# Wide units of a two-block transformer kernel: the 512-column matmuls with the high weights first, then the 256-column matmuls with the low weights

## The chip, the cores and the metric

The kernel runs on one core of a Trainium2 chip, as one launch. The metric is the device time of that launch in microseconds (us), read as the median of several runs. The kernel before took 1072.92 us (median of 3 runs, 1071.69 to 1077.14).

## What is computed

Two blocks follow each other on a sequence of 256 tokens of width 1024, all in float32. The first has a convolution and neighbourhood attention side by side, an output projection and a gated feed-forward part. The second has two layers, each with attention over selected keys, a short convolution, gates, a mixing projection and a squared-ReLU feed-forward part. The parts that matter here are the feed-forward ones:

```python
def first_block(...):
    ...
    x = x + mix @ w_out[l]
    h = rms_norm(x, norm2_g[l])
    x = x + (jax.nn.silu(h @ w_gate[l]) * (h @ w_up[l])) @ w_down[l]   # 1024 -> 2816 -> 1024
    return x

def second_block(...):
    for l in range(DEPTH_2):                                          # 2 layers
        ...
        x = x + merged @ w_mix_out[l]
        u = rmsnorm(x, norm_mlp[l])
        x = x + jnp.square(jax.nn.relu(u @ w_mlp_up[l])) @ w_mlp_down[l]   # 1024 -> 4096 -> 1024
    return rmsnorm(x, norm_final)
```

## The kernel before

**Units.** All weights pass through the core once, in units of 1 MB: 128 partitions by 2048 floats. SyncE's queue loads a unit into one of 6 buffers `raw`. ScalarE (ACT in the profile) rounds it to `whi` (L982, in the tensor engine's float32 format), and VectorE (DVE) subtracts that from the raw weights and writes the rest to `wlo` (L1289). Both have 3 buffers. A weight is then whi + wlo, and an activation is treated in the same way: `uhl` holds, for each of 8 feature chunks f, 256 columns of high parts (tokens, `uhi`) and behind them 256 columns of low parts (`ulo`). A product is the sum of three: high times high, high times low and low times high.

**Semaphores.** `w_hi` counts the units that ScalarE has split, `w_lo` those that VectorE has. `used` counts the units that the tensor engine (PE) has finished; ScalarE waits for it before it overwrites a buffer, three units later. A load waits for `w_lo` of the unit six before. `u_lo` counts the low parts of activation chunks.

**Kinds of units.** Most units are multiplied by three matmuls a step (`mm3`, L513 to L515). Where a unit has 256 output columns ("col" units) each matmul has 256 columns; in the output projections and in the second half of the feed-forward parts ("rows" units, `acc` banks) each has 512 columns, 24 matmuls a unit. A third kind, the **wide unit**, is used for gate and up projections: L541 multiplies `whi` by all 512 columns of `uhl` at once, which gives high times high in the left half of a bank and high times low in its right half, and L542 multiplies `wlo` by the 256 high columns into the left half. One unit is 2 output chunks c by 8 features f, so 16 pairs of such matmuls, in the order c, f, L541, L542. ScalarE then copies the right half out and VectorE adds the left one.

There are 54 wide units, 864 pairs. In the first block units `A_FF` and `A_FF + 1` are gate and up of the first 256 hidden features; then `ff_block` runs ten times (gate, up, and a rows unit `down`), and a last rows unit follows. In each of the two layers `L_MLP` is the first wide unit, and `block` runs 15 times (a wide unit `up` and a rows unit `down`).

**Where a feed-forward part starts.** The first wide unit of each (`wide_features_after`) is multiplied while the normed activations are still being made: the tensor engine transposes a quarter of x (`turn_quarter`, L609), ScalarE scales and rounds it (L999), and VectorE makes its low part (L1314), 4 chunks a quarter. The last quarter is transposed after the first four features of chunk c = 0, and features 4 to 7 wait for `u_lo`. The next work of ScalarE is the split of the next unit or two, then the sums of squares (L1011). In the first block, the second wide unit has in its middle, between c = 0 and c = 1, the four matmuls of `spread_rn` (L636). They wait for `diag_ok` of VectorE, which stands behind ScalarE's square root, and behind VectorE's splits of two units.

Every engine takes its work in the written order. The waits of a wide unit in the kernel before are at its callers, ahead of all its matmuls:

```python
                pe.wait_ge(w_lo, gate.upto())
                pe.wait_ge(ff_g, 2 * turns + q + 1)
                wide_features(gate, 0)
```

Of the kernel before, what the change touches and what calls it, by code (L numbers as in the profile page):

```python
# [22 lines left out]
P = 128  # L23
D = 1024
T = 256
NT = T // P
KD = D // P
# [26 lines left out]
COLS = 256  # L54
# [4 lines left out]
A_OUT, A_FF = 10, 14  # L59
# [77 lines left out]
def build(nc, d):  # L137
# [14 lines left out]
    with ExitStack() as ctx:  # L152
        def sb(name, shape, dt=F32):
            return ctx.enter_context(nc.sbuf_tensor(name, shape, dt))

        def sem(name):
            return ctx.enter_context(nc.semaphore(name))
# [6 lines left out]
        uhl = sb("uhl", [P, KD, 2 * T], F32R)  # L164
# [70 lines left out]
        col = [wide[i // 2][:, i % 2, :] for i in range(4)]  # L235
# [4 lines left out]
        w_hi = sem("w_hi")  # L240
        w_lo = sem("w_lo")
        used = sem("used")
# [88 lines left out]
        def whi_v(u, n=COLS):  # L331
            return whi[:, u.buf, :].rearrange("p (k n) -> p k n", n=n)

        def wlo_v(u, n=COLS):
            return wlo[:, u.buf, :].rearrange("p (k n) -> p k n", n=n)
# [10 lines left out]
        def a_unit(j, turns=0):  # L346
            return Unit(j, turns)

        def l_unit(l, j, turns=0):
            return Unit(A_UNITS + j, L_UNITS // RING * l + turns)  # L350
# [33 lines left out]
        def feature_count(k, f):  # L384

            return chunk_count(k, 1 + 2 * (f // 4), f % 4)
# [6 lines left out]
        def mid(buf, s):  # L393

            return buf[:, 2 * s:2 * s + 2, :]
# [115 lines left out]
        def _(pe):  # L511
# [24 lines left out]
                        between()  # L536
                mm.then_inc(used, 1)

            def mm_wide(u, n, c, f, start, stop):
                cs = slice(c * P, c * P + P)  # L540
                pe.matmul(col[2 * n + c][:], whi_v(u)[:, f, cs], uhl[:, f, :], start=start, stop=False)  # L541
                return pe.matmul(col[2 * n + c][:, 0:T], wlo_v(u)[:, f, cs], uhl[:, f, 0:T], start=False, stop=stop)  # L542

            def wide_features(u, n, between=None):

                for c in range(COLS // P):
                    for f in range(KD):
                        mm = mm_wide(u, n, c, f, f == 0, f == KD - 1)
                    if c == 0 and between:
                        between()  # L550
                mm.then_inc(used, 1)

            def wide_features_after(k, u, n):

                for h in range(2):
                    for c in range(COLS // P):
                        for f in range(4 * h, 4 * h + 4):
                            if c == 0:
                                pe.wait_ge(u_lo, feature_count(k, f))
                            mm = mm_wide(u, n, c, f, f == 0, f == KD - 1)  # L560
                        if h == 0 and c == 0:
                            turn_quarter(k, 3)
                mm.then_inc(used, 1)

            def col_features_after(k, u, bank, ready=None):

# [26 lines left out]
            def rows(u, hi_in, lo_in, start, stop):  # L593

                rows_half(u, 0, hi_in, lo_in, start, stop)
                rows_half(u, 1, hi_in, lo_in, start, stop).then_inc(used, 1)

            def turn_quarter(k, i):

                t, h = QUARTERS[i]  # L600
                if isinstance(k, int) and k == 0:
                    pe.wait_ge(x_in[h], 16)
                else:
                    pe.wait_ge(x_new, quarter_count(k, i))
                for c in range(4):
                    f = 4 * h + c
                    if i >= 2 and c == 2:
                        pe.wait_ge(u_lo, chunk_count(k, i - 2, 3))
                    tr = pe.transpose(quarter_bank(i, c), x[:, t, f * P:f * P + P], ident[:])  # L609
                    if c % 2:  # L610
                        tr.then_inc(u_ps, 1)
# [20 lines left out]
            def spread_rn(bank, count):  # L632

                pe.wait_ge(diag_ok, count)
                for t in range(NT):
                    mm = pe.matmul(bank[:, t * P:t * P + P], ones[:], diag[:, t, :], start=True, stop=True)  # L636
                mm.then_inc(rb_ps, 1)
# [101 lines left out]
            for j in range(A_OUT):  # L739
                u = a_unit(j)  # L740
# [26 lines left out]
                if j == 7 or j == 8:  # L767
                    n = j - 7
# [4 lines left out]
            for p in range(HEADS // 2):  # L773
# [10 lines left out]
                elif p == 2:  # L784
                    pe.wait_ge(conv_sb, KA)
                    for c in range(KA):
                        mm = pe.matmul(MU[:, 0:T], ones[:], y[:, c, :], start=c == 0, stop=c == KA - 1)
                    mm.then_inc(ln_mu, 1)
                else:
                    pe.wait_ge(ln_sq, 2)  # L790
                    for c in range(KA):
                        mm = pe.matmul(VAR[:, 0:T], ones[:], lnsq[:, c, :], start=c == 0, stop=c == KA - 1)
# [3 lines left out]
            u, r = a_unit(A_OUT), A_OUT_ROWS[0]  # L796
# [6 lines left out]
            u, r = a_unit(A_OUT + 1), A_OUT_ROWS[1]  # L803
# [6 lines left out]
            last_rows([(a_unit(A_OUT + 2), mhi[:, 0:2, :], mlo[:, 0:2, :]),  # L810
                       (a_unit(A_OUT + 3), mhi[:, 2:4, :], mlo[:, 2:4, :])], 1, conv_rows)

            pe.wait_ge(w_lo, a_unit(A_FF).upto())
            wide_features_after(1, a_unit(A_FF), 0)
            pe.wait_ge(w_lo, a_unit(A_FF + 1).upto())
            wide_features(a_unit(A_FF + 1), 1, lambda: spread_rn(acc[3], 2))
            pe.wait_ge(rb_sb, 2)

            def ff_block(q, turns, start):
                gate, up, down = (a_unit(A_FF + 2 + 3 * q + r, turns) for r in range(3))  # L820

                pe.wait_ge(w_lo, gate.upto())
                pe.wait_ge(ff_g, 2 * turns + q + 1)
                wide_features(gate, 0)
                pe.wait_ge(w_lo, up.upto())
                pe.wait_ge(ff_ok, 2 * turns + q + 1)
                wide_features(up, 1)
                pe.wait_ge(w_lo, down.upto())
                pe.wait_ge(ff_lo, 2 * turns + q + 1)
                rows(down, mid(mhi, q), mid(mlo, q), start, False)  # L830

            for q in range(2):
                ff_block(q, 0, q == 0)
            with pe.Fori(1, LOOPS) as i:
                for q in range(2):
                    ff_block(q, i, False)
# [30 lines left out]
            with pe.Fori(0, LAYERS) as l:  # L867

                first_units(l)
                for j in range(1, L_CONV):  # L870
                    u = l_unit(l, j)
# [29 lines left out]
                    if j == 4:  # L901
                        pe.wait_ge(idx_T, 2 * l + 2)
                        pe.wait_ge(rb_sb, 3 + l)
                        for h in range(IDX_HEADS):
                            off = 64 * (h % 2)
                            for t in range(NT):
                                mm = pe.matmul(acc[h][:, t * T:t * T + T], iqT[off:off + 64, h // 2, t * P:t * P + P],
                                               ikT[off:off + 64, :], start=True, stop=True)
# [17 lines left out]
                for i in range(4):  # L926
                    u = l_unit(l, L_CONV + i)
# [7 lines left out]
                for i in range(4):  # L935
                    u = l_unit(l, L_ATTN + i)
# [5 lines left out]
                for i in range(4):  # L942
                    u = l_unit(l, L_MIX + i)
# [4 lines left out]
                last_rows([(l_unit(l, L_MIX + 2), uhi[:, 4:6, :], ulo[:, 4:6, :]),  # L948
                           (l_unit(l, L_MIX + 3), uhi[:, 6:8, :], ulo[:, 6:8, :])], 3 + 2 * l)
                u = l_unit(l, L_MLP)  # L950
                pe.wait_ge(w_lo, u.upto())
                wide_features_after(3 + 2 * l, u, 0)

                def block(q, turns, done, start=False):
                    up, down = l_unit(l, L_MLP + 1 + 2 * (q % 3), turns), l_unit(l, L_MLP + 2 + 2 * (q % 3), turns)
                    pe.wait_ge(w_lo, up.upto())
                    wide_features(up, (1 + q) % 2)
                    pe.wait_ge(w_lo, down.upto())
                    pe.wait_ge(ff_lo, done + 1)
                    rows(down, mid(mhi, q % 3), mid(mlo, q % 3), start, False)  # L960

                done = FF_BLOCKS + MLP_BLOCKS * l
                for q in range(3):
                    block(q, 0, done + q, q == 0)
                with pe.Fori(0, 2) as i:
                    for q in range(6):
                        block(3 + q, 2 * i + 1 + q // 3, done + 6 * i + 3 + q)
# [836 lines left out]
```

## Time and profile before

| | |
|---|---|
| median of 3 runs | 1072.92 us (1071.69 to 1077.14) |
| the profiled execution | 1077.12 us |
| its span | 1075.3 us |
| PE busy with matmuls | 1044.9 us (97%) |
| DVE busy | 708.1 us (66%) |
| ACT busy | 538.7 us (50%) |
| mean share of the DMA engines in q1 | 54.4% |
| mean granted clock of the tensor engine | 0.996 of full speed |

The span is the time from the first to the last instruction in the profile; the execution's own time is 1.8 us longer. Busy times are sums of what the instructions of an engine took, without double counting. PE matmuls are pipelined: a matmul's listed duration is longer than the step from its start to the start of the next, so the step is what has to be read.

### The profile page before, as it was taken

The numbers are of one execution on the slowest core, as the hardware profiler recorded it, in microseconds if no ns is written. First come the engines' busy times: TensorE is split into PE (matmuls) and PEld (weight loads), VectorE is DVE, ScalarE is ACT, GpSimd is POOL, SyncE is SP. The second block draws the span as 40 slices with busy tenths as digits, with TensorE's granted clock in tenths as the row PEclk, the third lists the DMA queues.
The fourth block names the chain that finished last, engine by engine and source line by source line (L and its number), as shares of the span: only waits on it lengthen the run. The fifth ranks groups of instructions, "written<-read, shape, count | busy, mean of one in ns | idle before, by whom it ended". The sixth has DMA issues, their size and how long they took to land.

```text
span 1075.3 us, 17550 instructions
## 1 busy us (share of the span) xinstructions
PE 1044.9 (97%) x6689; PEld 921.8 (86%) x6689; DVE 708.1 (66%) x1073; ACT 538.7 (50%) x707; POOL 69.6 (6%) x80
## 2 busy tenths in 40 slices
PE   8989989999998999999999999999999999999997
PEld 6975778888888999998788888799999987888886
DVE  5886767666667576768666656466877676665654
ACT  6555565444446544455634444375354546444433
POOL 0000000000000308000000000002080000000000
PEclk9999999999999999999999999999999999999999
DMA  9974335555475564149465563765532674656520
GB/s 284 204 241 161 118 119 196 196 191 194 132 219 169 160 179 137 61 166 299 140 205 187 186 205 93 232 189 162 161 116 79 209 262 151 201 179 212 159 95 39
DMA packets 141922, 185.21 MB, mean 172 GB/s; under 512 B 6409, under 2 KB 126879, under 8 KB 141855
## 3 DMA queue, kind: packets, MB, share of 16 engines
q1 hardware_dynamic: 141767, 184.25, 54.4%
q8 instruction: 45, 0.74, 0.3%
q14 instruction: 22, 0.18, 0.1%
q10 hardware_dynamic: 88, 0.04, 0.0%
HBM read 180.91 MB, written 1.56 MB: 170 GB/s over the span
## 4 chain that ended last, share of the span: by engine, by line
PE 87%; DVE 3%; ACT 3%; SPq 2%; DMA 2%; issue 2%; ACTq 0%; DVEq 0%
PE wide L541 17%; PE wide L513 10%; PE wide L515 9%; PE wide L514 9%; PE acc L513 9%; PE acc L514 9%; PE acc L515 9%; PE wide L542 8%; ACT whi L982 2%; DVE wlo L1289 1%; DMA raw<-in_w_in 1%; SPq L434 1%; PE acc L674 1%; PE acc L708 1%; PE acc L695 1%
## 5 line engine op out<-in xcount | busy, mean ns | idle before, releaser
L1289 DVE TENSOR_TENSOR wlo<-raw,whi 128x2048 fp32r<-128x2048 f32 (+1 forms) x178 | 386.8, 2180 | 164.2 <-ACT whi L982 163.2
L982 ACT ACTIVATE whi<-raw 128x2048 fp32r<-128x2048 f32 (+1 forms) x178 | 322.3, 1818 | 97.5 <-PE wide L515 44.7
L541 PE MATMUL wide<-uhl,whi 128*128 128x512 f32 x864 | 307.7, 399 | 4.4 <-DVE wlo L1289 4.4
L542 PE MATMUL wide<-uhl,wlo 128*128 128x256 f32 x864 | 242.4, 281 | 0.0
L541 PEld LDWEIGHTS wide<-uhl,whi 128*128 128x128 f32 x864 | 162.4, 188 | 44.9 <-DVE wlo L1289 5.7
L542 PEld LDWEIGHTS wide<-uhl,wlo 128*128 128x128 f32 x864 | 163.3, 189 | 1.4
L513 PE MATMUL wide<-uhl,whi 128*128 128x256 f32 (+1 forms) x528 | 152.5, 289 | 0.8 <-DVE wlo L1374 0.8
L514 PE MATMUL wide<-uhl,whi 128*128 128x256 f32 (+1 forms) x528 | 150.3, 285 | 0.0
L515 PE MATMUL wide<-uhl,wlo 128*128 128x256 f32 (+1 forms) x528 | 150.2, 285 | 0.0
L513 PE MATMUL acc<-whi,mhi 128*128 128x512 f32 x376 | 147.8, 393 | 1.8 <-DVE wlo L1289 1.6
L514 PE MATMUL acc<-wlo,mhi 128*128 128x512 f32 x376 | 146.8, 390 | 0.0
L515 PE MATMUL acc<-whi,mlo 128*128 128x512 f32 x376 | 146.6, 390 | 0.0
L513 PEld LDWEIGHTS wide<-uhl,whi 128*128 128x128 f32 (+1 forms) x528 | 101.4, 192 | 2.9 <-issue 1.7
L514 PEld LDWEIGHTS wide<-uhl,whi 128*128 128x128 f32 (+1 forms) x528 | 101.4, 192 | 0.0
L515 PEld LDWEIGHTS wide<-uhl,wlo 128*128 128x128 f32 (+1 forms) x528 | 101.4, 192 | 0.0
L513 PE MATMUL wide<-whi,uhl 128*128 128x256 f32 x320 | 92.0, 288 | 2.8 <-DVE wlo L1289 2.8
L515 PE MATMUL wide<-whi,uhl 128*128 128x256 f32 x320 | 90.6, 283 | 0.0
L514 PE MATMUL wide<-wlo,uhl 128*128 128x256 f32 x320 | 90.6, 283 | 0.0
L513 PEld LDWEIGHTS acc<-whi,mhi 128*128 128x128 f32 x376 | 70.6, 188 | 18.4 <-issue 2.6
L515 PEld LDWEIGHTS acc<-whi,mlo 128*128 128x128 f32 x376 | 70.6, 188 | 15.3
L514 PEld LDWEIGHTS acc<-wlo,mhi 128*128 128x128 f32 x376 | 70.6, 188 | 13.2
L1255 ACT ACTIVATE xn<-wide 128x512 f32<-128x512 f32 x32 | 19.1, 597 | 104.2 <-PE wide L542 104.2
(251 smaller groups left out, 1288.1 us busy)
## 6 DMA issues: line engine op xcount, KB each, us to landing
raw<-in_w_in SPq DMA_DIRECT2D x51, 1024.0 KB, 5.4
raw<-in_w_mlp_up SPq DMA_DIRECT2D x32, 1024.0 KB, 6.0
raw<-in_w_mlp_down SPq DMA_DIRECT2D x32, 1024.0 KB, 4.9
raw<-in_w_gate SPq DMA_DIRECT2D x11, 1024.0 KB, 5.4
raw<-in_w_up SPq DMA_DIRECT2D x11, 1024.0 KB, 5.4
raw<-in_w_down SPq DMA_DIRECT2D x11, 1024.0 KB, 5.5
raw<-in_w_mix_out SPq DMA_DIRECT2D x8, 1024.0 KB, 6.0
raw<-in_w_out SPq DMA_DIRECT2D x4, 1024.0 KB, 8.2
```

Of the source, the lines that this page charges most:

```text
L434: sp.dma_start(into[:, :, q, :], cu[SHIFT_CH * q:SHIFT_CH * q + SHIFT_CH, 2 * half:2 * half + 2, s:s + SHIFTED])\
L513: pe.matmul(out, l_hi, r_hi, start=start, stop=False)
L514: pe.matmul(out, l_hi, r_lo, start=False, stop=False)
L515: return pe.matmul(out, l_lo, r_hi, start=False, stop=stop)
L541: pe.matmul(col[2 * n + c][:], whi_v(u)[:, f, cs], uhl[:, f, :], start=start, stop=False)
L542: return pe.matmul(col[2 * n + c][:, 0:T], wlo_v(u)[:, f, cs], uhl[:, f, 0:T], start=False, stop=stop)
L674: mm = pe.matmul(S_BANK[e][:, t * T:t * T + n], qT[off:off + DH, p, t * P:t * P + P], kT[off:off + DH, p, 0:n], start=True, stop=not isins ...
L695: tr = pe.transpose(t_bank(a, h)[:, kt * T + t * P:kt * T + t * P + P], expo[h % 4][:, t, kt * P:kt * P + P], ident[:])
L708: mm = pe.matmul(O_BANK[off:off + DH, t0:T], vtok[:, kt, h * DH:h * DH + DH], prob[:, e, kt * T + t0:kt * T + T], start=kt == 0, stop=kt = ...
L982: act.activation(whi[:, u.buf, 0:size], raw[:, u.slot, 0:size], ACT.Copy).then_inc(w_hi, 1)
L1255: act.activation(mlp_h[s].rearrange("p (c t) -> p c t", c=2), wide[n][:, :, T:2 * T], ACT.Copy).then_inc(ff_act, 1)
L1289: dve.tensor_tensor(wlo[:, u.buf, 0:size], raw[:, u.slot, 0:size], whi[:, u.buf, 0:size].bitcast(F32), ALU.subtract).then_inc(w_lo, 1)
```

## The change

In a wide unit all 16 matmuls of 512 columns with the high weights (L541) come first, then all 16 of 256 columns with the low weights (L548 in the changed file). The first group waits for `w_hi` alone, and the second group for `w_lo`. The sums in a bank are the same, added in another order. `used` is still counted by the last matmul. The diff is complete but for unchanged lines.

```diff
-            def mm_wide(u, n, c, f, start, stop):
-                cs = slice(c * P, c * P + P)
-                pe.matmul(col[2 * n + c][:], whi_v(u)[:, f, cs], uhl[:, f, :], start=start, stop=False)
-                return pe.matmul(col[2 * n + c][:, 0:T], wlo_v(u)[:, f, cs], uhl[:, f, 0:T], start=False, stop=stop)
+            def wide_high(u, n, c, f):
+
+                pe.matmul(col[2 * n + c][:], whi_v(u)[:, f, c * P:c * P + P], uhl[:, f, :], start=f == 0, stop=False)
+
+            def wide_low(u, n):
+
+                pe.wait_ge(w_lo, u.upto())
+                for c in range(COLS // P):
+                    for f in range(KD):
+                        mm = pe.matmul(col[2 * n + c][:, 0:T], wlo_v(u)[:, f, c * P:c * P + P], uhl[:, f, 0:T],
+                                       start=False, stop=f == KD - 1)
+                mm.then_inc(used, 1)
 
             def wide_features(u, n, between=None):
 
+                pe.wait_ge(w_hi, u.upto())
                 for c in range(COLS // P):
                     for f in range(KD):
-                        mm = mm_wide(u, n, c, f, f == 0, f == KD - 1)
+                        wide_high(u, n, c, f)
                     if c == 0 and between:
                         between()
-                mm.then_inc(used, 1)
+                wide_low(u, n)
 
             def wide_features_after(k, u, n):
 
+                pe.wait_ge(w_hi, u.upto())
                 for h in range(2):
                     for c in range(COLS // P):
                         for f in range(4 * h, 4 * h + 4):
                             if c == 0:
                                 pe.wait_ge(u_lo, feature_count(k, f))
-                            mm = mm_wide(u, n, c, f, f == 0, f == KD - 1)
+                            wide_high(u, n, c, f)
                         if h == 0 and c == 0:
                             turn_quarter(k, 3)
-                mm.then_inc(used, 1)
+                wide_low(u, n)
...
-            pe.wait_ge(w_lo, a_unit(A_FF).upto())
             wide_features_after(1, a_unit(A_FF), 0)
-            pe.wait_ge(w_lo, a_unit(A_FF + 1).upto())
             wide_features(a_unit(A_FF + 1), 1, lambda: spread_rn(acc[3], 2))
...
-                pe.wait_ge(w_lo, gate.upto())
                 pe.wait_ge(ff_g, 2 * turns + q + 1)
                 wide_features(gate, 0)
-                pe.wait_ge(w_lo, up.upto())
                 pe.wait_ge(ff_ok, 2 * turns + q + 1)
                 wide_features(up, 1)
...
                 u = l_unit(l, L_MLP)
-                pe.wait_ge(w_lo, u.upto())
                 wide_features_after(3 + 2 * l, u, 0)
...
-                    pe.wait_ge(w_lo, up.upto())
                     wide_features(up, (1 + q) % 2)
```

The order on PE in a layer's feed-forward loop, around the start of a wide unit (bank pair wide0) behind a rows unit (acc3). REGISTER_ALU works out a number that a wait compares with. Before:

```order
2763 L515 MATMUL acc3<-whi,mlo 128x512
2764 L956 REGISTER_ALU
2765 L541 MATMUL wide0<-uhl,whi 128x512 [waits w_lo]
2766 L542 MATMUL wide0<-uhl,wlo 128x256
2767 L541 MATMUL wide0<-uhl,whi 128x512
2768 L542 MATMUL wide0<-uhl,wlo 128x256
```

After:

```order
2439 L515 MATMUL acc3<-whi,mlo 128x512
2440 L554 REGISTER_ALU
2441 L541 MATMUL wide0<-uhl,whi 128x512 [waits w_hi]
2442 L541 MATMUL wide0<-uhl,whi 128x512 x15
2443 L548 MATMUL wide0<-uhl,wlo 128x256 [waits w_lo]
2444 L548 MATMUL wide0<-uhl,wlo 128x256 x15
```

The 16 alternating pairs have become a run of 16 and a run of 16, and the wait for `w_lo` has moved from the unit's first matmul to its seventeenth.

The order on PE in unit `A_FF + 1`, the second wide unit of the first block, around `spread_rn` (acc3<-rtmp,ones). Before:

```order
752 L541 MATMUL wide1<-uhl,whi 128x512
753 L542 MATMUL wide1<-uhl,wlo 128x256
754 L636 MATMUL acc3<-rtmp,ones 128x128 [waits diag_ok]
755 L636 MATMUL acc3<-rtmp,ones 128x128
756 L541 MATMUL wide1<-uhl,whi 128x512
757 L542 MATMUL wide1<-uhl,wlo 128x256
```

After:

```order
713 L541 MATMUL wide1<-uhl,whi 128x512 [waits w_hi]
714 L541 MATMUL wide1<-uhl,whi 128x512 x7
715 L646 MATMUL acc3<-rtmp,ones 128x128 [waits diag_ok]
716 L646 MATMUL acc3<-rtmp,ones 128x128
717 L541 MATMUL wide1<-uhl,whi 128x512 x8
718 L548 MATMUL wide1<-uhl,wlo 128x256 [waits w_lo]
719 L548 MATMUL wide1<-uhl,wlo 128x256 x15
```

Ahead of the wait for `diag_ok` there are now 8 matmuls of 512 columns, where there were those 8 and 8 of 256.

## Rows read from the trace of the kernel before

**Rows 1.** The page: the span, PE's busy time, and the granted clock in 40 slices.

```profile
span 1075.3 us, 17550 instructions
...
PE 1044.9 (97%) x6689; PEld 921.8 (86%) x6689; DVE 708.1 (66%) x1073; ACT 538.7 (50%) x707; POOL 69.6 (6%) x80
...
PEclk9999999999999999999999999999999999999999
```

**Rows 2.** Groups by line and shape, PE: count | busy us, mean ns | idle before.

```profile
L541 PE MATMUL wide<-uhl,whi 128*128 128x512 f32 x864 | 307.7, 399 | 4.4 <-DVE wlo L1289 4.4
L542 PE MATMUL wide<-uhl,wlo 128*128 128x256 f32 x864 | 242.4, 281 | 0.0
```

**Rows 3.** Timeline of PE, one wide unit's start and the next unit's: start us, duration us.

```profile
557.40 0.39 PE L541 MATMUL wide<-uhl,whi 128*128 128x512 f32 x1
...
563.04 0.40 PE L513 MATMUL acc<-whi,mhi 128*128 128x512 f32 x1
```

**Rows 4.** Timeline of PE, a rows unit (24 matmuls of 512 columns) and its successor.

```profile
498.03 0.39 PE L513 MATMUL acc<-whi,uhl 128*128 128x512 f32 x1
...
503.47 0.39 PE L513 MATMUL acc<-whi,uhl 128*128 128x512 f32 x1
```

**Rows 5.** Timeline of PE, a col unit (24 of 256 columns), its successor, a rows unit.

```profile
486.80 0.28 PE L513 MATMUL wide<-mhi,whi 128*128 128x256 f32 x1
...
489.68 0.28 PE L513 MATMUL wide<-mhi,whi 128*128 128x256 f32 x1
...
492.56 0.40 PE L513 MATMUL acc<-whi,uhl 128*128 128x512 f32 x1
```

**Rows 6.** Waits of PE: us in total, times, longest.

```profile
PE wide L541 <- DVE wlo L1289: 4.4, 4, 1.5
```

**Rows 7.** Timeline of PE, start of the first block's feed-forward part.

```profile
134.91 0.48 PE L541 MATMUL wide<-uhl,whi 128*128 128x512 f32 x1
...
136.41 0.60 PE L609 MATMUL acc<-ident,x 128*128 128x128 f32 x4
...
142.15 0.50 PE L541 MATMUL wide<-uhl,whi 128*128 128x512 f32 x1 [0.90 <-DVE wlo L1289]
...
146.02 0.71 PE L636 MATMUL acc<-rtmp,ones 128*128 128x128 f32 x4 [0.82 <-DVE rtmp L1337]
...
149.39 0.40 PE L541 MATMUL wide<-uhl,whi 128*128 128x512 f32 x1
...
156.73 0.49 PE L541 MATMUL wide<-uhl,whi 128*128 128x512 f32 x1 [1.53 <-DVE wlo L1289]
...
162.39 0.39 PE L513 MATMUL acc<-whi,mhi 128*128 128x512 f32 x1
```

**Rows 8.** Timeline of ACT, same stretch.

```profile
136.83 1.14 ACT L999 ACTIVATE uhl<-acc,gcol 128x128 fp32r<-128x128 f32 x4 [0.72 <-PE acc L609]
137.84 3.74 ACT L982 ACTIVATE whi<-raw 128x2048 fp32r<-128x2048 f32 x2
...
152.45 3.70 ACT L982 ACTIVATE whi<-raw 128x2048 fp32r<-128x2048 f32 x2
```

**Rows 9.** Timeline of DVE, same stretch.

```profile
137.49 1.13 DVE L1314 SCALAR_TENSOR_TENSOR uhl<-acc,gcol,uhl 128x128 fp32r<-128x128 f32 x4 [0.73 <-ACT uhl L999]
...
154.39 4.49 DVE L1289 TENSOR_TENSOR wlo<-raw,whi 128x2048 fp32r<-128x2048 f32 x2 [1.11 <-ACT whi L982]
```

**Rows 10.** Timeline of PE, start of the first layer's feed-forward part.

```profile
515.67 0.48 PE L541 MATMUL wide<-uhl,whi 128*128 128x512 f32 x1
...
522.90 0.50 PE L541 MATMUL wide<-uhl,whi 128*128 128x512 f32 x1 [0.97 <-DVE wlo L1289]
...
529.60 0.49 PE L513 MATMUL acc<-whi,mhi 128*128 128x512 f32 x1 [0.79 <-DVE wlo L1289]
```

**Rows 11.** Timeline of ACT and of DVE, same stretch.

```profile
522.48 0.60 ACT L1255 ACTIVATE xn<-wide 128x512 f32<-128x512 f32 x1
...
527.18 4.49 DVE L1289 TENSOR_TENSOR wlo<-raw,whi 128x2048 fp32r<-128x2048 f32 x2 [1.11 <-ACT whi L982]
```

More of the change, by code:

```diff
@@ L537, in col_features, with wide_features @@
                 mm.then_inc(used, 1)
-            def mm_wide(u, n, c, f, start, stop):
-                cs = slice(c * P, c * P + P)
-                pe.matmul(col[2 * n + c][:], whi_v(u)[:, f, cs], uhl[:, f, :], start=start, stop=False)
-                return pe.matmul(col[2 * n + c][:, 0:T], wlo_v(u)[:, f, cs], uhl[:, f, 0:T], start=False, stop=stop)
-            def wide_features(u, n, between=None):
+            def wide_high(u, n, c, f):
+                pe.matmul(col[2 * n + c][:], whi_v(u)[:, f, c * P:c * P + P], uhl[:, f, :], start=f == 0, stop=False)
+            def wide_low(u, n):
+                pe.wait_ge(w_lo, u.upto())
                 for c in range(COLS // P):
                     for f in range(KD):
-                        mm = mm_wide(u, n, c, f, f == 0, f == KD - 1)
+                        mm = pe.matmul(col[2 * n + c][:, 0:T], wlo_v(u)[:, f, c * P:c * P + P], uhl[:, f, 0:T],
+                                       start=False, stop=f == KD - 1)
+                mm.then_inc(used, 1)
+            def wide_features(u, n, between=None):
+                pe.wait_ge(w_hi, u.upto())
+                for c in range(COLS // P):
+                    for f in range(KD):
+                        wide_high(u, n, c, f)
                     if c == 0 and between:
                         between()
-                mm.then_inc(used, 1)
+                wide_low(u, n)
             def wide_features_after(k, u, n):
+                pe.wait_ge(w_hi, u.upto())
                 for h in range(2):
```

## The prediction

> **What bounds the kernel now.** I read the page first: of a span of 1075.3 us the tensor engine (PE) is busy with matmuls for 1044.9 us, and its granted clock is at its upper level (2.4 GHz) in all 40 slices [rows 1]. So the kernel is PE-bound nearly everywhere. Two things can make it faster: a shorter step from one matmul to the next, or the end of one of the few idle stretches. The groups by line give the size of what is touched: 864 pairs in 54 wide units, with 4.4 us of idle time in front of them, all of it released by VectorE's low split of weights [rows 2]. The view of waits says the same and adds that it is four waits, the longest 1.5 us [rows 6]. The listed durations (399 and 281 ns) overlap, so for the steps I went to the timeline.
>
> **The change, part by part.**
>
> *The step between matmuls.* One wide unit starts at 557.40 and its successor at 563.04: 5.64 us for 16 pairs, 352.5 ns a pair [rows 3]. What would the same matmuls take in runs of one size? A unit of 24 matmuls of 512 columns takes 503.47 - 498.03 = 5.44 us, 226.7 ns each [rows 4]. One of 24 matmuls of 256 columns takes 489.68 - 486.80 = 2.88 us, 120 ns each [rows 5]. Sixteen of each make 3.627 + 1.920 = 5.547 us. Alternating two sizes thus costs 0.093 us a unit more than running them apart. There is a small price where a run of 512 columns follows one of 256: the rows unit at 492.56 behind a col unit ends at 498.03, 5.47 us instead of 5.44 [rows 4, 5]. In a layer every wide unit follows a rows unit, whose matmuls have 512 columns, so it pays nothing new, and the rows unit behind it follows a 256-column matmul as before. In the first block an `up` unit follows the low run of its `gate` unit and pays the 0.03: I give it 0.07 instead of 0.093.
>
> The Trainium skill (TensorE: Matmul & The Clock Gate, "Wait — 56ns, not 53.3ns?") puts the step between warm matmuls at the column count divided by 2.4 GHz plus about 2.5 ns, whatever stands next to them. By it a pair would take 325 ns in either order and the reordering would bring nothing. The trace agrees neither with its size (352.5 against 325) nor with the sum of its own two uniform runs (346.7); I take the rows, and keep the rule as a rival.
>
> *Number of gaining units.* The first four wide units of the first block and the first two of each layer are treated below by place. Left are 9 blocks in the first block, with a `gate` and an `up` each: 9 x (0.093 + 0.07) = 1.47 us. In each of the two layers 14 of 16 wide units are left: 28 x 0.093 = 2.60 us. In these stretches PE never waits, so each saving is one of the span. Sum: **4.07 us**. The bounds: 46 x 0 if alternation is not what costs, 46 x 0.10 = 4.6 us.
>
> *Start of the first block's feed-forward part* [rows 7 to 9]. Before, the first wide unit runs from 134.91, with the last transposes at 136.41, to about 141.1. The second starts at 142.15 (late low split), meets `spread_rn` at 146.02 (0.8 us late), and ends at 149.39. The third, `gate`, ends at about 155.05, and `up` starts at 156.73, 1.5 us late. The rows unit starts at 162.39.
> After: four high matmuls instead of four pairs precede the transposes, so these come 4 x 0.12 = 0.5 to 0.6 us earlier (x has its last quarter by then), and ScalarE's and VectorE's work behind them with it: 136.83 becomes 136.25, 137.49 becomes 136.9. But only four high matmuls (0.91 us, not 1.4) now stand between the transposes and feature 4, whose low part is ready at about 137.2. PE gets there at 137.25 and is then paced for three features by VectorE (1.13 us for 4 chunks, 0.28 each against PE's 0.227), a loss of 0.2 us. The unit ends at 141.15, as before.
> ScalarE's two splits start at 137.25 instead of 137.84, so `w_hi` of the second unit is there at 139.1: its high half starts at once at 141.15, 1.0 us earlier. Eight matmuls later, at 143.0, PE stands before `spread_rn`, and VectorE is ready for that only at about 145.4 (145.97 before, earlier by the same 0.6). The wait grows from 0.8 to 2.4 us, and the eight low matmuls that stood ahead of it (0.96 us) now stand behind it. 145.43 + 0.47 + 1.82 + 1.92 gives 149.65: this unit ends 0.25 us **later** than before. So here the removed wait comes back in full at the next one.
> `gate` then runs to 155.2. `up` needs `w_hi` only, and ScalarE has it at 152.45 + 1.85 = 154.3; the low split is at 154.39 + 2.25 = 156.65, well before PE asks at 158.9. `up` ends at 160.8 instead of 162.39. The rows unit needs both splits: the second low split ends at 158.88. Gain of this start: **1.6 us**, of which some 0.3 is the shorter step.
>
> *Start of each layer's feed-forward part* [rows 10, 11]. The same pattern: the first unit from 515.67 ends at 521.9 (521.8 before); the second starts there, because its high split has been ready since 520.5 or earlier (the low split, about 2.25 us long, followed it and ended just before 522.90), and not at 522.90; it ends at 527.45 instead of 528.66. But behind it stands a rows unit, which needs the low split of its weights, and that was late already: VectorE's split of 527.18 ends at 529.47, and PE starts at 529.60 with 0.8 us of idle time. What sets it is ScalarE's L1255 at 522.48 (it waits behind the squares, and for the end of the first unit), the square, the mid split, and the two weight splits behind them. Of these ScalarE's part moves up with the earlier transposes, until L1255 is bound by the first unit's end: 522.14 instead of 522.48. So **0.35 us** per layer is gained, and the rest of the 1.2 us becomes a longer wait at 529. Two layers: 0.7 us; bounds 0 and 1.2.
>
> *Added waits.* PE waits 54 times more, in the middle of a unit. Such waits stand on the weight load of the matmul behind them. The col unit at 486.80 and its successor at 489.68 each begin with satisfied waits, one of them for `w_lo`, and the 2.88 us from the one to the other are 24 steps of 120 ns with nothing on top [rows 5], so I take 0. The far bound is the 0.1 us by which the matmul behind a wait that really stopped PE is listed longer (0.50 against 0.40, [rows 3, 7]), if it were paid at every wait: 54 x 0.1 = 5.4 us. In steady state the low split of a unit is done long before its high half ends, since before the change it was done before the unit began. Buffers are released at the unit's end as before, and the loads, which hang on `w_lo`, are untouched.
>
> *Sum:* 4.07 + 1.6 + 0.7 = 6.4 us. Against the profiled execution's 1077.1 us that is 1070.7. That execution is 4.2 us slower than the median of the runs; on the median, 1072.92 - 6.4 = **1066.5 us** (-0.6%). A measurement of this kernel can tell some 0.5%, or 5.4 us, from no change, so the forecast lies just beyond what can be told.
>
> **The rivals.**
> 1. *Steps do not depend on the order*, the rule of the skill's page above, read as a mechanism of this kernel: the 353 ns a pair belongs to two streams with 512- and 256-column reads of `uhl`, and stays when they are apart. For it: no stretch of this trace has runs of either size with wide operands. Against it: the uniform runs cover four pairs of operands, all alike. Then only the idle time at the starts goes: 1.3 + 0.7 = 2.0 us, 1070.9 us.
> 2. *The added wait costs where it is satisfied* 0.08 us each: 54 x 0.08 = 4.3 off the 6.4, 1070.8 us. Against it is the col unit above, whose wait costs nothing.
> 3. *Slower: the low run is bound by weight loads.* Its 16 loads are all of new weights, where in the runs of 256 columns before two of three matmuls in a row use the same ones. PE's weight loads are busy 921.8 us for 6689 of them, 138 ns each [rows 1], overlapping the matmuls. If each step of the run took 138 ns instead of 120, a unit would take 16 x 0.018 = 0.29 us more: 54 x 0.29 = 15.6 against 6.4, 1082 us. The point from which it decides is a step of 127.4 ns (6.4 / 864 = 7.4 above 120). Against it: the steps of the col unit are 120 for all three kinds of pairs.
> 4. *The gains at the starts are lost*: `spread_rn` or the paced features cost more than I find, and 4 us are left: 1068.9 us.
>
> That the change does not do what it says can be left out: the order of the instructions shows it.
>
> **How the numbers follow.** My forecast 0.65, rival 1 0.14, rival 2 0.10, rival 3 0.05, rival 4 0.06. The forecast's own spread is about 1 us in its terms (5.3 to 7.4) and about 2 us from the median of a few runs (3 runs here lie within 5.5 us). Of its 0.65 some 0.53 lies beyond 5.4 us; with scatter of the others 0.03 more. Faster 0.56, same 0.39, slower 0.05. The range runs from 1063.0 (7.4 and a low median) to 1072.0 (rivals 1 and 2 and 1 us of scatter), and leaves out rival 3 and the far ends.
>
> **What the profile after would show.** The 512-column steps within a unit at 227 ns and the 256-column ones at 120, a layer's wide unit at 5.55 us instead of 5.64; no wait for the low split in front of L541; a wait of about 2.4 us at `spread_rn` instead of 0.8; a wait of about 1.8 us instead of 1.0 in front of the first rows unit of each layer. Wrong would be: a wide unit of 5.64 us (rival 1), a gap in front of the first low matmul of every unit (rival 2), low steps above 127 ns (rival 3), or rows units that start no earlier than before after the first block's start (rival 4).

## The result, and the profile after

The changed kernel takes 1070.25 us (median of 19 runs, 1067.45 to 1072.71); the kernel before took 1075.38 us (median of 19 runs, 1071.69 to 1079.48, the three that the forecast was counted from among them). The ratio is 0.9947, with a 95% interval of 0.9936 to 0.9957: 5.7 us faster, or 0.53% (4.6 to 6.9 us by the interval; the two medians lie 5.1 us apart). The forecast was 6.4 us.

The page of the changed kernel, first its span and clock, then its groups by line (busy us, mean ns of one | idle before):

```profile
span 1065.7 us, 17542 instructions
...
PE 1040.3 (98%) x6689; PEld 923.8 (87%) x6689; DVE 708.1 (66%) x1073; ACT 538.6 (51%) x707; POOL 69.6 (7%) x80
...
PEclk8999999999999999999999999999999999999999
...
L541 PE MATMUL wide<-uhl,whi 128*128 128x512 f32 x864 | 208.5, 393 | 0.0
...
L513 PE MATMUL acc<-whi,mhi 128*128 128x512 f32 x376 | 147.6, 392 | 3.2 <-DVE wlo L1293 2.9
...
L548 PE MATMUL wide<-uhl,wlo 128*128 128x256 f32 x864 | 112.1, 283 | 0.0
```

The idle time in front of L541, 4.4 us before [rows 2], is gone, and there is 2.9 us of waiting for `wlo` in front of the rows units. The busy figures of the two groups (L541 and L542, now L541 and L548) fell from 307.7 and 242.4 us to 208.5 and 112.1, which is no gain of that size: overlapping time is counted once within a group, and in pairs each matmul's listed duration overlapped one of the other group. PE's own busy time fell by 4.6 us only [rows 1].

The two profiled executions differ by 9.6 us of span, more than the runs do. So I compare stretches, each from one start on PE to another. The timeline of PE after has at the places of [rows 7]:

```profile
130.68 1.18 PE L541 MATMUL wide<-uhl,whi 128*128 128x512 f32 x4
131.69 0.60 PE L619 MATMUL acc<-ident,x 128*128 128x128 f32 x4
132.04 3.33 PE L541 MATMUL wide<-uhl,whi 128*128 128x512 f32 x12
...
137.12 2.00 PE L541 MATMUL wide<-uhl,whi 128*128 128x512 f32 x8
141.31 1.22 PE L646 MATMUL acc<-rtmp,ones 128*128 128x128 f32 x4 [2.18 <-DVE rtmp L1341]
142.19 3.19 PE L541 MATMUL wide<-uhl,whi 128*128 128x512 f32 x8
147.12 3.82 PE L541 MATMUL wide<-uhl,whi 128*128 128x512 f32 x16
152.69 3.82 PE L541 MATMUL wide<-uhl,whi 128*128 128x512 f32 x16
158.26 0.40 PE L513 MATMUL acc<-whi,mhi 128*128 128x512 f32 x1
```

And at those of [rows 3, 10], the start of the first layer's feed-forward part and one wide unit in its steady part:

```profile
509.87 1.18 PE L541 MATMUL wide<-uhl,whi 128*128 128x512 f32 x4
...
516.32 3.82 PE L541 MATMUL wide<-uhl,whi 128*128 128x512 f32 x16
...
523.50 0.49 PE L513 MATMUL acc<-whi,mhi 128*128 128x512 f32 x1 [1.45 <-DVE wlo L1293]
...
551.08 3.79 PE L541 MATMUL wide<-uhl,whi 128*128 128x512 f32 x16
554.70 2.08 PE L548 MATMUL wide<-uhl,wlo 128*128 128x256 f32 x16
556.62 0.40 PE L513 MATMUL acc<-whi,mhi 128*128 128x512 f32 x1
```

| stretch | before | after | measured | forecast |
|---|---|---|---|---|
| first block's start, first wide unit to first rows unit | 162.39 - 134.91 = 27.48 | 158.26 - 130.68 = 27.58 | +0.1 | -1.6 |
| from there to the next transposes (9 blocks, 18 wide units) | 162.05 | 160.07 | -2.0 | -1.5 |
| start of a layer's part, first wide unit to first rows unit, two layers | 529.60 - 515.67 = 13.93 | 523.50 - 509.87 = 13.63 | 2 x -0.3 | 2 x -0.35 |
| a layer's wide unit in the steady part, 28 of them | 5.64 | 556.62 - 551.08 = 5.54 | 28 x -0.10 | 28 x -0.093 |

Three things stand out. The steady units gained a little more than forecast. The starts of the layers gained what was forecast. And the first block's start, where 1.6 us were expected, gained nothing.

What happened there shows in the granted clock. The view by windows, of the changed kernel (us of the window, busy time of PE, of the weight loads, DVE, ACT and POOL, then PEclk):

```profile
138.00:141.00 3.00, 1.13 (x5) 0.58 (x4) 1.98 (x4) 2.51 (x4) 0.00 (x0) 1.00 0.82 224
141.00:144.50 3.50, 3.19 (x10) 2.71 (x11) 1.18 (x4) 1.91 (x3) 0.00 (x0) 0.52 1.05 377
145.00:147.00 2.00, 2.00 (x17) 1.96 (x16) 0.69 (x1) 0.62 (x1) 0.00 (x0) 1.00 0.00 1
```

and of the kernel before, around its shorter wait for the same four matmuls:

```profile
144.00:146.00 2.00, 1.20 (x8) 0.79 (x6) 0.95 (x4) 1.25 (x2) 0.00 (x0) 1.00 1.00 389
146.00:149.00 3.00, 2.98 (x18) 2.65 (x19) 1.22 (x2) 2.15 (x3) 0.00 (x0) 1.00 1.06 377
```

Before `spread_rn` (L636, now L646) PE is idle for 2.18 us, where it was 0.82 [rows 7]. Right behind it the clock is at half (1.2 GHz). The eight matmuls of 512 columns from 142.19 on and the sixteen of 256 behind them take 147.12 - 142.19 = 4.93 us; 8 x 0.227 + 16 x 0.12 at full clock would be 3.74. With the four of `spread_rn`, 0.88 us instead of 0.47, the half clock costs 1.6 us. (A profile below has the same matmuls at full clock with the change of size in them; against that one it is 1.5 us.)

### The profile page after: what moved, and what is told of

Read it like the earlier page. It is cut to its first block, busy times and chain, and to the rows that moved or that the text cites. A ratio compares the mean times of both kernels' runs of the same rounds, so it can differ in the third digit from the quotient of the medians.

```text
span 1065.7 us, 17542 instructions
## 1 busy us (share of the span) xinstructions
PE 1040.3 (98%) x6689; PEld 923.8 (87%) x6689; DVE 708.1 (66%) x1073; ACT 538.6 (51%) x707; POOL 69.6 (7%) x80
## 4 chain that ended last, share of the span: by engine, by line
PE 89%; DVE 3%; SPq 2%; ACT 2%; DMA 2%; issue 1%; ACTq 0%; DVEq 0%
PE wide L541 17%; PE wide L513 10%; PE wide L514 10%; PE wide L515 10%; PE acc L513 9%; PE acc L514 9%; PE acc L515 9%; PE wide L548 9%; DMA raw<-in_w_in 1%; DVE wlo L1293 1%; SPq L434 1%; ACT whi L986 1%; PE acc L684 1%; PE acc L718 1%; PE acc L705 1%
## 5 line engine op out<-in xcount | busy, mean ns | idle before, releaser
L541 PE MATMUL wide<-uhl,whi 128*128 128x512 f32 x864 | 208.5, 393 | 0.0
L541 PEld LDWEIGHTS wide<-uhl,whi 128*128 128x128 f32 x864 | 161.4, 189 | 33.9 <-DVE uhl L1318 1.2
L548 PEld LDWEIGHTS wide<-uhl,wlo 128*128 128x128 f32 x864 | 110.8, 191 | 4.3
L548 PE MATMUL wide<-uhl,wlo 128*128 128x256 f32 x864 | 112.1, 283 | 0.0
```

The costliest lines, as they stand in the source:

```text
L541: pe.matmul(col[2 * n + c][:], whi_v(u)[:, f, c * P:c * P + P], uhl[:, f, :], start=f == 0, stop=False)
L548: mm = pe.matmul(col[2 * n + c][:, 0:T], wlo_v(u)[:, f, c * P:c * P + P], uhl[:, f, 0:T], start=False, stop=f == KD - 1)
```

## The experiments

All of these were timed against the kernel before in the same way. Where a stretch is called "the first block's start" here, it is counted from the first transposes (134.56 before) to the first rows unit: 27.83 us before, 27.94 after.

### The same kernel again

No edit.

> The changed kernel once more. In its first profile the tensor engine stood idle for 2.6 us before spread_rn and its granted clock then was 0.5 for 3.4 us, so that the stretch from the last transposes before A_FF to the first rows unit took 27.94 us, no less than before (27.83). Theory 1 (the fall of the clock belongs to that wait): in this profile too the clock is at 0.5 from about 141 us on (counted as in the first profile) and the stretch takes 27.8 to 28.0 us. Rival (it was an accident of that execution): the clock stays full there and the stretch takes 26.2 to 26.4 us. Both: 4 to 7 us faster than before in all.

Measured: ratio 0.995 (0.9935 to 0.9966). The stretch takes 27.98 us. Timeline and windows of PE in this second profile:

```profile
138.88 2.00 PE L541 MATMUL wide<-uhl,whi 128*128 128x512 f32 x8
143.07 0.71 PE L646 MATMUL acc<-rtmp,ones 128*128 128x128 f32 x4 [2.19 <-DVE rtmp L1341]
143.53 3.43 PE L541 MATMUL wide<-uhl,whi 128*128 128x512 f32 x8
```

```profile
139.50:142.50 3.00, 1.38 (x7) 0.79 (x5) 2.01 (x2) 2.77 (x6) 0.00 (x0) 1.00 0.63 202
143.00:146.50 3.50, 3.43 (x12) 2.81 (x13) 1.40 (x3) 2.42 (x4) 0.00 (x0) 0.63 1.05 368
```

The same wait and again the half clock behind it, begun one microsecond later: `spread_rn` itself ran at full speed (0.71), and the low run behind the high half bears the rest. The fall is no accident of one execution; where it begins is: 0.16 us before `spread_rn` starts in the first profile, 0.86 us behind its start in the second.

### The new order with the old wait

```diff
             def wide_low(u, n):
-                pe.wait_ge(w_lo, u.upto())
...
             def wide_features(u, n, between=None):
-                pe.wait_ge(w_hi, u.upto())
+                pe.wait_ge(w_lo, u.upto())
...
             def wide_features_after(k, u, n):
-                pe.wait_ge(w_hi, u.upto())
+                pe.wait_ge(w_lo, u.upto())
```

> The new order, but the old wait: both runs of a wide unit wait for w_lo ahead of the unit, so no unit starts early. Step theory (the gain is the step between matmuls, 0.10 us a wide unit in 46 units): a layer's wide unit takes 5.54 us, and the kernel is about 3.9 us faster than before, 1.2 to 1.5 us slower than the changed kernel, since only the start of the first block's up unit is lost. Early-start theory (the gain comes from waiting for the high split alone): most of the 5 us is lost here, the kernel within 1.5 us of before.

Measured: 0.9954 (0.9939 to 0.997). A layer's wide unit takes 5.54 us. The start of the first block takes 28.14 us, 0.2 more than in the changed kernel and not 1.2 to 1.5: the `up` unit waits again, but the idle time before `spread_rn` is shorter and the clock stays up (1.00 in the windows from 140 to 148).

```profile
139.42 2.11 PE L541 MATMUL wide<-uhl,whi 128*128 128x512 f32 x8 [0.16 <-DVE wlo L1292]
143.29 0.71 PE L645 MATMUL acc<-rtmp,ones 128*128 128x128 f32 x4 [1.76 <-DVE rtmp L1340]
143.76 2.09 PE L541 MATMUL wide<-uhl,whi 128*128 128x512 f32 x8
...
154.79 3.91 PE L541 MATMUL wide<-uhl,whi 128*128 128x512 f32 x16 [1.46 <-DVE wlo L1292]
```

So the gain of the change is that of the order. The early wait, as it was put in, is worth nothing measurable: what it gives at `up` (1.46 us of waiting gone) the half clock takes. The starts of the layers say the same: 13.63 us in this profile, as in the changed kernel. And the order by itself lengthens the first block's start, by 0.3 us (27.83 before), since the eight low matmuls that stood ahead of `spread_rn` now stand behind it.

### spread_rn behind both high halves

```diff
                     for f in range(KD):
                         wide_high(u, n, c, f)
-                    if c == 0 and between:
-                        between()
+                if between:
+                    between()
                 wide_low(u, n)
```

> The changed kernel, with the four matmuls of spread_rn behind both high halves of unit A_FF + 1 instead of between them. Theory (the longer wait at spread_rn, 2.6 us, and the half clock behind it eat the gain of the first block's start): the wait falls to 0.4 to 0.8 us, the clock stays full, the low run ends at 143.7 instead of 147.1, and with w_hi of the up unit as the next bound the stretch from the transposes before A_FF to the first rows unit takes 24.9 us instead of 27.9; in all 3 us faster than the changed kernel. Rival (what bounds there is the chain of ScalarE and VectorE behind it, whatever the tensor engine does): the stretch stays above 27 us and the kernel equals the changed one.

Measured: 0.9929 (0.9908 to 0.995). The first block's start takes 25.45 us, 2.5 less than in the changed kernel (3.0 expected):

```profile
136.17 3.82 PE L541 MATMUL wide<-uhl,whi 128*128 128x512 f32 x16
140.35 0.71 PE L646 MATMUL acc<-rtmp,ones 128*128 128x128 f32 x4 [0.37 <-DVE rtmp L1341]
143.59 3.91 PE L541 MATMUL wide<-uhl,whi 128*128 128x512 f32 x16 [0.62 <-issue]
```

The wait is down to 0.37 us and the clock stays at 1.00. The second row with idle time (0.62) is `gate`, which starts 0.6 us after PE could: it needs `ff_g`, the gating of the first pair, and `rb_sb`, ScalarE's copy of what `spread_rn` makes. The copy and the work behind it moved less than PE did: counted from the first transposes, PE was done with unit `A_FF + 1` 3.4 us earlier than in the changed kernel, while the copy began only 0.52 us earlier, and so did the end of the gating, at 143.49. This is the half microsecond by which the expectation was too high. The rival, that VectorE's and ScalarE's chain hides all of it, falls.

### Filling the idle time with work

```diff
-            wide_features(a_unit(A_FF + 1), 1, lambda: spread_rn(acc[3], 2))
+            wide_features(a_unit(A_FF + 1), 1, lambda: (keep_warm(10, acc[2]), spread_rn(acc[3], 2)))
```

> The changed kernel, with ten matmuls of zeros (512 columns, bfloat16, into bank acc2, which nobody needs then; nothing of the result changes) between the first high half of A_FF + 1 and spread_rn, 10 x 0.216 = 2.16 us, so about as long as the idle time there. Theory (idle time lets the clock fall): the granted clock stays 1.0 there, spread_rn starts at the same moment as without them, the second high half takes 1.8 us instead of 2.8, and the stretch to the first rows unit takes 26.3 us instead of 27.9; in all 1.6 us faster than the changed kernel. Rival (the clock falls for another reason, or its fall is hidden by the wait of the up unit for its high split): the stretch stays within 0.3 us of 27.9.

Measured: 0.9938 (0.9916 to 0.9959), an interval that overlaps the changed kernel's. So this rests on the trace. The first block's start takes 26.42 us, and the clock does not fall there (of the ten matmuls of zeros the trace has nine; they step by 0.216 us):

```profile
139.88 2.00 PE L541 MATMUL wide<-uhl,whi 128*128 128x512 f32 x8
141.95 2.11 PE L651 MATMUL acc<-zeros 128*128 128x512 bf16 x9
144.07 0.71 PE L646 MATMUL acc<-rtmp,ones 128*128 128x128 f32 x4
144.53 2.09 PE L541 MATMUL wide<-uhl,whi 128*128 128x512 f32 x8
```

```profile
142.00:144.00 2.00, 2.00 (x9) 0.74 (x8) 0.98 (x4) 1.29 (x2) 0.00 (x0) 1.00 0.96 377
144.00:147.00 3.00, 2.99 (x18) 2.60 (x18) 1.19 (x3) 2.15 (x3) 0.00 (x0) 1.00 1.05 375
```

Useless matmuls make the stretch 1.5 us shorter. They change nothing for the other engines, and `spread_rn` still waits for its cause; only the idle time is gone: it starts 10.99 us behind the first transposes in both kernels. That shows what the fall costs, about 1.5 us, and that without the idle time it did not come. It is one profile, though, and the length of an idle stretch alone does not tell whether the clock falls. This same profile has a longer wait elsewhere, with the clock at 1.00 behind it:

```profile
57.73 1.50 PE L745 MATMUL acc<-big,cB 128*32 128x256 f32 x24 [3.16 <-DMA big<-cu]
```

And a wait of 1.98 us for ScalarE's `prob`, which stands at 101 to 106 us in all nine profiles, was followed by a half clock of 3.4 us in three of them (`after_again`, `order_only`, `starts_only`). What else decides was not tried and stays open.

The filled kernel also tells what the early wait is worth once the clock stays up: 28.14 - 26.42 = 1.7 us against the new order with the old wait.

### Groups of four

A wide unit alternates between four matmuls of 512 columns and four of 256; all wait for `w_lo` ahead, as in the second experiment.

```diff
...
                 for c in range(COLS // P):
-                    for f in range(KD):
-                        wide_high(u, n, c, f)
+                    for g in range(0, KD, 4):
+                        for f in range(g, g + 4):
+                            wide_high(u, n, c, f)
+                        for f in range(g, g + 4):
+                            mm = low_one(u, n, c, f)
...
```

(`low_one` is one matmul of 256 columns with the low weights. The first wide unit of each feed-forward part keeps its two runs.)

> As order_only (all waits on w_lo ahead of the unit), but a wide unit alternates in groups: 4 matmuls of 512 columns, then 4 of 256, four times, so 7 changes of size within a unit instead of 31 (pairs) or 1 (runs). Settling theory (each return to 512 columns costs some 25 ns over the next five matmuls, and the 256-column ones behind a change win back 8): a layer's wide unit takes 5.60 us, between 5.64 (pairs) and 5.54 (runs). Rival (each change costs the same, 0.10 us over 30 changes, 3.3 ns): 5.56 us. In all 1.3 us (rival) to 3 us (settling) slower than order_only.

Measured: 0.998 (0.9961 to 0.9998). One unit, from a layer's steady part:

```profile
554.41 1.07 PE L541 MATMUL wide<-uhl,whi 128*128 128x512 f32 x4
555.32 0.64 PE L554 MATMUL wide<-uhl,wlo 128*128 128x256 f32 x4
...
560.00 0.40 PE L513 MATMUL acc<-whi,mhi 128*128 128x512 f32 x1
```

It takes 5.59 us, and the rows unit behind it 5.49 instead of the changed kernel's 5.47, so 0.07 us more than in runs. That is between the two theories' 5.56 and 5.60, nearer the settling one once the rows unit is counted. It confirms that the price is one of changing the size, paid less often the longer the runs are. Which of the two forms it has is not settled by 0.01 us, nor by the runs: the two ratios (0.998 here, 0.9954 for `order_only`) lie 2.8 us apart, but their intervals touch.

The same profile says something on the wait at `spread_rn`. Here and in `order_only` everything waits for `w_lo`, but here the eight low matmuls of c = 0 stand ahead of `spread_rn` again, and the wait is back at its length of before, 0.80 us against 1.76:

```profile
144.30 0.71 PE L654 MATMUL acc<-rtmp,ones 128*128 128x128 f32 x4 [0.80 <-DVE rtmp L1349]
```

The first block's start takes 27.46 us, 0.4 less than before and 0.7 less than in `order_only`. So the grown wait is made of moved cover: 8 x 0.12 = 0.96 us.

### The new order at the starts alone

```diff
-                wide_features(gate, 0)
+                (wide_features if start else wide_pairs)(gate, 0)
...
-                wide_features(up, 1)
+                (wide_features if start else wide_pairs)(up, 1)
...
-                    wide_features(up, (1 + q) % 2)
+                    (wide_features if start else wide_pairs)(up, (1 + q) % 2)
```

(`wide_pairs` is the old unit: pairs, with the wait for `w_lo` ahead.)

> The new order with the early wait only in the first four wide units of the first block and the first two of each layer; all others alternate in pairs and wait for w_lo ahead, as before. Step theory (most of the gain is the shorter step in the steady blocks): the wide units of the loops take 5.64 us again, the starts are as in the changed kernel (0.1 us lost in the first block with the clock's fall, 0.3 us gained in each layer), and the kernel is 0.5 to 1.0 us faster than before, 4.5 us slower than the changed one. Early-start theory: it keeps more than 2.5 us of the changed kernel's 5.

Measured: 0.9988 (0.9978 to 0.9998), some 1.3 us faster than before (0.2 to 2.4 by the interval; 0.9 by the profile, from the first wide unit to the end). The steady units take 5.64 us again, the first block's start 28.00 us, and the half clock is there for the third time:

```profile
143.00:146.00 3.00, 1.09 (x5) 0.56 (x3) 1.98 (x4) 2.47 (x4) 0.00 (x0) 1.00 0.83 242
146.20:149.70 3.50, 3.44 (x11) 2.86 (x12) 1.40 (x3) 2.15 (x3) 0.00 (x0) 0.55 1.05 369
```

The early-start theory falls: it wanted more than 2.5 of the 5 us here.

### High weights first in a rows unit as well

`spread_late`, and the first rows unit of each layer's feed-forward part waits for `w_hi`, multiplies all that needs `whi` (16 matmuls), waits for `w_lo`, and multiplies the rest (8). The cut is of the new function alone; its call and the edit of `spread_late` are left out.

```diff
...
+            def rows_early(u, hi_in, lo_in, start):
+                pe.wait_ge(w_hi, u.upto())
+                for low in range(2):
+                    for q in range(4):
+                        t, h = q // 2, q % 2
+                        tok, cs = slice(t * P, t * P + P), slice(h * 512, h * 512 + 512)
+                        for c in range(2):
+                            if low:
+                                mm = pe.matmul(acc[q][:], hi_in[:, c, tok], wlo_v(u, D)[:, c, cs], start=False, stop=False)
+                            else:
+                                pe.matmul(acc[q][:], hi_in[:, c, tok], whi_v(u, D)[:, c, cs], start=start and c == 0, stop=False)
+                                pe.matmul(acc[q][:], lo_in[:, c, tok], whi_v(u, D)[:, c, cs], start=False, stop=False)
+                    if not low:
+                        pe.wait_ge(w_lo, u.upto())
+                mm.then_inc(used, 1)
```

> spread_late, and in addition the first rows unit of each layer's feed-forward part waits for w_hi alone: its 16 matmuls that read whi come first, then a wait for w_lo, then the 8 that read wlo. Theory (the rest of the gain of each layer's start went into the wait for that unit's low split, 1.7 us with what the tensor engine pays behind it): that wait is gone, because w_hi is there 0.9 us before the tensor engine asks and w_lo comes during the first 16; each layer gains 1.6 to 1.7 us, the kernel 3.3 us on spread_late, 11 us on before. Rival (the wait moves on to the next unit, whose split follows in the same queue): less than 1 us on spread_late.

Measured: 1063.36 us (median of 4 runs), 0.9883 (0.9867 to 0.9899), 12.6 us faster than before and the fastest of all. PE at the start of the first layer's feed-forward part:

```profile
516.74 3.82 PE L541 MATMUL wide<-uhl,whi 128*128 128x512 f32 x16
520.39 2.08 PE L548 MATMUL wide<-uhl,wlo 128*128 128x256 f32 x16
522.31 0.40 PE L619 MATMUL acc<-whi,mhi 128*128 128x512 f32 x1
...
525.96 1.98 PE L617 MATMUL acc<-wlo,mhi 128*128 128x512 f32 x8
527.77 3.79 PE L541 MATMUL wide<-uhl,whi 128*128 128x512 f32 x16
```

No idle time is left, neither at 522.31 nor at 525.96, and the next wide unit starts without a wait. From the start of the second wide unit to that of the third, with the first rows unit between them, it takes 527.77 - 516.74 = 11.03 us; in the changed kernel it is 529.06 - 516.32 = 12.74. That is 1.7 us in this layer, and the second layer shows the same, as expected. The rival, that the wait moves on, falls.

## Why the prediction was right, and where it was not

**The step between matmuls** was read rightly. A wide unit in runs takes 5.54 us, where 16 x 226.7 + 16 x 120 ns gave 5.547. The starts-only and order-only kernels show it from both sides: with pairs in the steady part nearly all of the gain is gone, with the order alone nearly all of it is there. The term was a little small, 4.07 us against 1.98 + 28 x 0.10 = 4.8: the unit gained 0.100 instead of 0.093, and each `down` unit of the first block 0.036 us, which I had not counted. Rival 1, that the 353 ns a pair stay when the two sizes are apart, falls. The rule beside it, from the Trainium skill (TensorE: Matmul & The Clock Gate, "Wait — 56ns, not 53.3ns?"), that each warm matmul steps by its columns at 2.4 GHz and a fixed 2.5 ns, does not fit these weights and activations in any order: 346.7 ns for the sum of a step in each run, where it gives 325.

**The added waits** cost nothing. Units with the wait in their middle and units without one (`order_only`) both take 5.54 us. Rival 2 falls.

**The low run** keeps its 120 ns a step; rival 3 falls.

**The layers' starts** went as forecast in the main: the earlier transposes, the second unit at once behind the first, and most of the gain turned into a longer wait for the low split of the rows unit (1.45 us, 0.79 before [rows 10]). `rows_early` shows that this was all that held it. What the forecast had too small is the pacing by VectorE's low parts: five steps behind the last transposes take 0.34 to 0.35 us (two) and 0.25 to 0.26 (three) instead of 0.227, which is 0.3 us, where 0.2 was written. The first block's first unit has the same steps.

**The first block's start** is the step that failed: "145.43 + 0.47 + 1.82 + 1.92 gives 149.65". The wait was forecast well (from the last matmul's start to the next it is 2.57 us, less its own step of 0.23 that is 2.34, where I had written 2.4; the profile lists 2.18 as idle), and that the removed wait would come back at `spread_rn` was right. But what stands behind the wait was priced at full clock. In all three profiles with this wait the clock fell to half around its end, in the first of them the matmuls from `spread_rn` to the end of the unit took 5.81 us instead of 0.47 + 1.82 + 1.92 = 4.2, and the stretch gained nothing instead of 1.6 us. I had counted 1.6 us for this place in the sum, and 0.06 for rival 4, which names a loss of about this size there, but through paced features or the wait itself.

**The sum.** 6.4 forecast; without the 1.6 and with 0.7 more from the steps it would be 5.5. From the first wide unit to the end the two profiles differ by about 5.4 us. So the total came out nearer than its parts: a term of 1.6 us that was lost was in part made up by steps that gave more than was counted, and that is luck. Two smaller items are in the 5.4 and were not foreseen. At the jump back from layer 1 to layer 2, PE takes its first transposes 0.38 us sooner behind the last matmul than in the profile before (0.23 us against 0.62), and 0.27 to 0.38 sooner in the other changed kernels; why was not tried and stays open. And in the profile after, the clock was at half for 3.4 us once more, around 322 us, where PE waits for activations at the start of a layer, and that cost 0.3 us; the second profile has such a fall at the start of the other layer instead (0.8 us), and one more at 103 us (1.6 us). The profile of the kernel before has one at 57 us, for 3.4 us, which the digits of PEclk in [rows 1] do not show, since a 9 stands for 90% or more. Such falls come in some executions and not in others, and are likely a part of the scatter of the runs.

The forecast median of 1066.5 us was off by 3.8 us, where the gain was off by 0.7, since the median of the three runs that it was counted from (1072.92) lay 2.5 us below that of all nineteen (1075.38).

## What to carry to other kernels

Read the step between matmuls from a long run of one size and from the alternating stretch; where the sum of the uniform steps is smaller, sorting the matmuls by size saves the difference, as long as what stands ahead of a later wait still covers it. Work that needs the first half of a pair of buffers can start on that half's semaphore, but then look what the engine meets next: cover that is moved behind a later wait makes that wait longer, and on the tensor engine idle time can cost twice, once for itself and once for the half clock behind it. A wait that can't be shortened is better met late, behind work that doesn't depend on it (2.5 us here), or filled with useless matmuls (1.5 us here).

## What the runs showed of the hardware

- Changing between 512 and 256 columns of the moving operand costs: in pairs 352.5 ns, in runs 226.7 + 120 = 346.7 ns. A unit of 512-column matmuls behind a run of 256 is 0.03 us longer [rows 4, 5].
- At `spread_rn` an idle stretch of PE of 2.2 us went with a granted clock of 0.5 in three of three profiles, and waits of 1.8 us and less in the same place in none of the five others (in `warm_fill` there is none). The loss was 1.5 to 1.6 us. Elsewhere it is mixed: 3.16 us without a fall in `warm_fill`, 1.98 us with one in three of nine profiles. The Trainium skill (TensorE: Matmul & The Clock Gate, "What's actually happening") says that the throttled clock is the default and activity releases it; the trace of `warm_fill` agrees as far as one profile can, as ten matmuls of zeros kept it at 1.00, and in the profile after it was back at 1.00 by 145.00, with the matmuls running.
- The profiled executions differ by up to 6 us before the first changed instruction, in part by a wait for a DMA of the convolution, 2.6 us before and 0.9 us after. A saving of 5 us can't be read from two spans, but it can from stretches of the trace, most of which repeat within 0.02 us where the clock is full (the nine blocks of the first feed-forward part take 160.07 us in all six profiles with sorted units).
